# Mixer of a transformer block on one core: VectorE's reciprocal of a chunk's sums, and where it stands against the end of the chunk in front

## The reference, cut to what matters

```python
v = to_heads(dv, N_DIFF_HEADS)
a1 = causal_block_attention(q1, k1, v)
a2 = causal_block_attention(q2, k2, v)
diff_o = a1 - lam.astype(a1.dtype) * a2
diff_o = rms_norm(diff_o, subln_g) * (1.0 - lam_init)
```

## Time and profile before

| | |
|---|---|
| median of three runs | 3871.53 us |
| profiled execution | 3867.04 us |
| its span | 3865.2 us |
| around the span | 1.84 us |
| TensorE busy | 3734.7 us (97%) |
| VectorE busy | 2372.4 us (61%) |
| ScalarE busy | 1653.8 us (43%) |
| GpSimd busy | 1693.8 us (44%) |
| mean granted TensorE clock | 0.987 |

### The profile page before, as it was taken

One profiled execution on the slowest core, in us unless ns is written; L12 is line 12 of the kernel. 1 busy time (PEld: TensorE's weight loads), 2 busy tenths in 40 slices (PEclk: granted clock), 3 DMA queues, 4 the chain that ended last, 5 costly groups with the idle time before them and its releaser, 6 DMA issues.

```text
span 3865.2 us, 50420 instructions
## 1 busy us (share of the span) xinstructions
PE 3734.7 (97%) x19892; PEld 3036.6 (79%) x19892; DVE 2372.4 (61%) x3104; ACT 1653.8 (43%) x2799; POOL 1693.8 (44%) x1112
## 2 busy tenths in 40 slices
PE   7999999999999898999999899999999999999998
PEld 5888888666655466888888799999879988888877
DVE  7667785633455548667684766644577156666663
ACT  5333344422222335333444454411572256666663
POOL 4555554244444544555553144422532233443464
PEclk9999999999999999999999999999999999999999
DMA  3334574200000122234574111221111300000024
GB/s 112 105 106 150 173 260 145 88 23 22 26 19 17 45 77 71 96 109 150 194 247 134 33 39 44 66 94 61 47 69 59 131 32 23 30 25 29 29 67 140
DMA packets 143405, 327.30 MB, mean 85 GB/s; under 512 B 16896, under 2 KB 20512, under 8 KB 142784
## 3 DMA queue, kind: packets, MB, share of 16 engines
q1 hardware_dynamic: 131280, 279.70, 21.8%
q0 software_dynamic: 9328, 41.75, 2.9%
q10 hardware_dynamic: 2560, 2.61, 0.2%
HBM read 252.37 MB, written 71.63 MB: 84 GB/s over the span
## 4 chain that ended last, share of the span: by engine, by line
PE 78%; DVE 13%; ACT 5%; POOL 2%; issue 2%; DMA 1%; SPq 0%; DVEq 0%; ACTq 0%; POOLq 0%
PE ps L955 6%; PE ps L956 6%; PE ps L957 6%; PE ps L415 5%; PE ps L416 5%; PE ps L417 5%; PE ps L4266 4%; PE ps L973 3%; PE ps L975 3%; PE ps L974 3%; PE ps L4198 2%; PE ps L2009 2%; PE ps L4200 2%; PE ps L4199 2%; PE ps L2011 2%; PE ps L2010 2%
## 5 line engine op out<-in xcount | busy, mean ns | idle before, releaser
L389 POOL TENSOR_TENSOR wlo<-raw,whi 128x1024 fp32r<-128x1024 f32 x154 | 376.4, 2448 | 483.6 <-ACT whi L380 483.5
L415 PE MATMUL ps<-xh,whi 128*128 128x352 f32 (+1 forms) x1400 | 473.4, 338 | 6.7 <-DVE xl L672 2.7
L416 PE MATMUL ps<-xh,wlo 128*128 128x352 f32 (+1 forms) x1400 | 450.8, 322 | 0.0
L417 PE MATMUL ps<-xl,whi 128*128 128x352 f32 (+1 forms) x1400 | 449.9, 321 | 0.0
L862 POOL TENSOR_TENSOR fwl<-fpb,fwh 128x512 fp32r<-128x512 f32 x204 | 302.7, 1494 | 265.7 <-ACT fwh L852 265.5
L862 POOL TENSOR_TENSOR fwl<-fpa,fwh 128x512 fp32r<-128x512 f32 x202 | 292.9, 1459 | 276.1 <-ACT fwh L852 276.1
L4571 POOL TENSOR_TENSOR ospl<-osp,osph 128x672 fp32r<-128x672 f32 (+4 forms) x144 | 191.0, 1326 | 359.1 <-ACT osph L4392 358.0
L415 PEld LDWEIGHTS ps<-xh,whi 128*128 128x128 f32 x1400 | 265.0, 189 | 18.2 <-POOL wlo L389 5.8
L416 PEld LDWEIGHTS ps<-xh,wlo 128*128 128x128 f32 x1400 | 264.6, 189 | 8.0 <-issue 2.2
L417 PEld LDWEIGHTS ps<-xl,whi 128*128 128x128 f32 x1400 | 264.4, 189 | 0.0
L955 PE MATMUL ps<-fxh,fwh 128*128 128x512 f32 x640 | 249.1, 389 | 1.3 <-ACT u L1033 1.3
(11 more groups left out here) (506 smaller groups left out, 9704.6 us busy)
## 6 DMA issues: line engine op xcount, KB each, us to landing
raw<-in_w_dram SPq DMA_DIRECT2D x154, 512.0 KB, 3.7
hs_scratch<-u SPq DMA_DIRECT2D x176, 256.0 KB, 2.4
u<-hs_scratch SPq DMA_DIRECT2D x118, 256.0 KB, 2.8
fpa<-in_fg_dram SPq DMA_DIRECT2D x88, 256.0 KB, 3.9
fpb<-in_fg_dram SPq DMA_DIRECT2D x88, 256.0 KB, 3.8
fpa<-in_fd_dram SPq DMA_DIRECT2D x88, 256.0 KB, 3.5
fpb<-in_fd_dram SPq DMA_DIRECT2D x88, 256.0 KB, 3.7
acc<-hs_scratch SPq DMA_DIRECT2D x80, 256.0 KB, 2.8
```

Source lines behind the costliest of these rows:

```text
L389: pool.x.tensor_tensor(K.wlo[n % 3][:, :], K.raw[n % 2][:, :], K.whi[n % 3][:, :], ALU.subtract).then_inc(*S.up("w_lo", n))
L415: pe.x.matmul(out, wh, xh, start=k == 0, stop=False)
L416: pe.x.matmul(out, wl, xh, start=False, stop=False)
L417: last = pe.x.matmul(out, wh, xl, start=False, stop=k == K - 1)
```

## The change

At s = 4 of heads 5, 6 and 7 the end of the chunk in front, `root` of (t-1, 1), is now in VectorE's list behind rec of (t, 0); before, it was at s = 3, ahead of it. VectorE now acts on a new entry `scale` where it acted on `root`. The entries of (t, 0) at s = 7 and of (7, 1) at the end keep their places. ScalarE's copy of the spread reciprocals to `mb` for (t, 0) now waits for the `root` of (t-1, 1), since that still uses the tile. No operation is added or taken away; TensorE's and GpSimd's instructions keep their order.

```diff
+        if s == 4 and t >= 5:
+            out.append(("scale", (t - 1, 1), 0))
...
         if e and e[0] == "var":
             out.append(("root", e[1], 0))
+            if e[1][1] == 0:
+                out.append(("scale", e[1], 0))
...
     out.append(("root", (7, 1), 0))
+    out.append(("scale", (7, 1), 0))
...
     def wide(t, c, r):
         act.wait_ge("pe_mix", ("wide", t, c))
+        if c == 0 and t >= 5:
+            act.wait_ge("dve_mix", ("root", t - 1, 1))
         act.x.activation(K.mb[:, :, :], two(K, 2 * r, 0, 512), ACT.Copy).then_inc(*S.up("act_mix", ("wide", t, c)))
...
-        elif what == "root":
+        elif what == "scale":
             root(*arg)
```

## The result

The changed kernel takes 3878.35 us (median of 19 runs, 3869.57 to 3887.73) against 3871.53 us (19 runs, 3866.59 to 3880.0). The ratio is 1.0021, 95% interval 1.0014 to 1.0028: slower by 5 to 11 us. The forecast was 3876.0 in a range of 3869 to 3881.

The account below looks back on a forecast made before the run. TensorE bounds the kernel (78% of the span); VectorE counts only where TensorE stands still for it. Heads 5, 6 and 7 give 3.7 + 2.5 - 1.7 = +4.5 us on 3871.53: median 3876.0 us, range 3869 to 3881 (8 in 10).

Parts of the forecast that it names:

- Root behind rec, 5.0 us: VectorE, heads 5 to 7: root's four operations take 5.0 us behind rec, the second blocked by GpSimd for 2.77.
- the lower bound: Root's four operations behind rec take 2.9 us if nothing collides with GpSimd.
- Head 5, wait +3.1: Head 5: ScalarE's copy starts behind root instead of at 1155.40, 3.1 us later, and the mix with it.
- Head 6, wait +2.45: Head 6: the mix starts at 1247.6 instead of 1245.14, 2.45 us later.
- Head 7, -1.7: Head 7: rec no longer stands behind root, so ScalarE's copy starts at 1319.7 instead of 1321.41, 1.7 us earlier.
- The new wait "costs nothing beyond what is counted": ScalarE's queue: what stands behind the waiting copy needs its result or later scores anyway, so no extra cost.
- The clock, +0.6 and +0.05: TensorE at 1.2 GHz behind the pause: the mix takes 3.46 us instead of 2.84 in head 5, 3.39 in head 6.
- rival B: Heads 5 and 6: half clock lasts 7.7 us behind each new pause, 2.1 us more twice; +8.7 us, 3880.2; chance 0.11.
- A delay at these places is not made up later: TensorE, heads 5 to 7: its work is fixed, in order, and its weights are there, so delays stay.
- Rival A: Heads 5 to 7: root runs free behind rec, 2.9 us at each place; -2.9 us, 3868.6; chance 0.12.
- Rival C: Only head 7 counts, the copy of heads 5 and 6 not held up; -1.7 us, 3869.8; chance 0.02.

Follow-up runs that it names:

- the experiment on it: Changed kernel with GpSimd's first sum of the second half waiting for root of the head in front in heads 5 to 7: 3869.78 us beside 3868.52 for before.
- the two moves of the head alone: Kernel before, with rec ahead of root and ScalarE's new wait in head 7 only: 3864.5 us beside 3869.65 for before.
- The filled waits: Changed kernel with six matmuls of constants, never read, in TensorE's wait for the banks in heads 5 and 6: 3870.42 us beside 3868.52 for before.

## Why the prediction was right

By its own steps, against the first profile of the changed kernel (start of its first rec 1.56 us later than before; taken off below):

- *Root behind rec, 5.0 us*: 4.93. The first operation free, the second blocked, the others free, in heads 5 and 6 word for word. Without the collision it is 2.9 (the experiment on it), as the lower bound said. Blocking, and not slowing, is what the traces bear out. From 1000 us on, the 13 profiles of the mixer have 124 operations of root that took 1.15 to 4.39 us instead of some 0.7, and every one ends 0.53 to 0.56 us behind the end of a GpSimd operation, however early it began; at a slower rate the distance would vary with the start. (Three more stand beside two GpSimd operations that the view merges into one row.)
- *Head 5, wait +3.1*: the mix starts 1162.57 - 1157.87 - 1.56 = 3.1 us later. Right.
- *Head 6, wait +2.45*: the work ahead of it is 5.5 us late at the sums and the mix 7.9. Right.
- *Head 7, -1.7*: -1.9 at the mix. Right; the two moves of the head alone are -1.7 there.
- *The new wait "costs nothing beyond what is counted"*: right, but it was only 1.2 of the 4.4 us, and the order on VectorE 2.4.
- *The clock, +0.6 and +0.05*: this is the term that was mis-sized. I ended the half clock with the mix. It went on through the scores: mix and scores took 5.64 us in head 5, where they took 3.9 before, +1.75 instead of +0.6; in head 6 5.7 instead of 4.5, +1.2; in head 7 +1.15, where I had nothing. That was rival B's mechanism at half its price. The filled waits show it: with VectorE's chain as late as in the changed kernel, 6.9 us came back. But the size holds for this pair of profiles only. In the second profile of before, mix and scores took 5.66, 3.96 and 5.18 us at the three places; against that one the clock's part is 2.2 us, not 4.1.
- *"A delay at these places is not made up later"*: wrong in head 7. 2.8 us came back behind its mix: root of (7, 0) met less of GpSimd's work (2.44 us instead of the 3.62 of the earlier trace rows) and TensorE's wait for the output split shrank from 2.07 to 0.89 us, with no half clock behind it now (a mix of 1.88 us, 3.03 before):

```profile
1351.83 0.50 PE L2035 MATMUL ps<-fxh,whi 128*128 128x512 f32 x1 [0.89 <-POOL fxl L2619]
...
1352.63 1.88 PE L2133 MATMUL ps<-mp,mvt 128*128 128x512 f32 x4
```

So +3.1 +2.4 -1.9 of waits, +4.1 of clock, -2.8 back, and some 1.1 us at the mixes behind the second halves' copies (3.78 us in head 7 where before had 3.49), give the 6.1; the forecast's +4.5 had the first three right and most of the clock missing. That its total came as near as it did is partly luck: 4.6 us that it left out (3.5 of clock, 1.1 at the other mixes) were offset in part by the 2.8 us that came back, which it had excluded.

Rival A (root free) fell: the collision came each time. Rival C fell with it. Between the forecast and B the time alone doesn't decide: 3878.35 is 2.4 us above the forecast's 3876.0 and 1.9 us below B's 3880.2. B's sign, slow scores behind the mix, did appear; its price of 7.7 us at half clock behind each pause didn't, it was 5.6 to 5.7.

## What to carry to other kernels

A reorder on an engine that isn't the bottleneck moves its work from ahead of one hand-over to ahead of the next one: look for the last hand-over of the chain and put the independent work behind that, here with a second tile, since the shared one forbade it. Price a pause of TensorE with the matmuls behind it, and expect that price to differ between executions; in the kernels that filled such pauses with matmuls whose result nobody reads, it was gone behind each filled one. When a chain gets shorter, look at once at the next place where it meets GpSimd: about half of the gain in the mixer waited there (6.0, then 12.7 us).

## What the runs showed of the hardware that I had not expected

- The half clock falls differently in two executions of one program: head 6's mix at 2.84 and at 1.98 us, head 4's at 1.98 and at 3.78, behind pauses of 0.6 to 0.9 us; and it can stay away behind a pause of 2.46 us. Once fallen at the mix behind a first half, it mostly lasted through mix and scores, 5.6 to 5.7 us for work of 3.0 us at full clock.
- A VectorE operation with both inputs in SBUF, begun at 1325.73 while GpSimd did nothing but issue DMAs (1323.93 to 1327.13), ended at 1330.12, 0.56 us behind GpSimd's sum of 1327.15 to 1329.56. Either the issuing blocked it already, or the sum got ahead of it though it began later. A place in the second block of the kernel before speaks for the latter: an operation with both inputs in SBUF took its usual 0.51 us while GpSimd issued one DMA. That was one issue, not six in a row, so it isn't proof. VectorE, then GpSimd:

```profile
2905.49 0.51 DVE L3846 SCALAR_TENSOR_TENSOR gv<-gv,gr 128x336 f32<-128x336 f32 x1
...
2905.34 0.88 POOL L4054 DMA_DIRECT2D res<-rs_scratch  x1 [17.98 <-DVE xl L3941]
```
